# ConvFFN of a two-layer encoder trunk: the down product as seven block products in a phase of its own

## The reference, cut to what matters

```
def conv_ffn(h, w_up, conv_w, conv_b, w_down):
    u = h @ w_up                                  # (1024, 1024) @ (1024, 5632)
    u = causal depthwise conv of width 3 over the tokens (u, conv_w) + conv_b
    gate, val = split(u, 2)                       # 2816 channels each
    return (silu(gate) * val) @ w_down            # (1024, 2816) @ (2816, 1024)
```

## Time and profile before

| | |
|---|---|
| median of three runs | 2635.62 us |
| span of the profiled execution, first to last instruction | 2631.1 us |
| PE busy | 2439.2 us, 93% of the span |
| DVE busy | 1926.0 us, 73% |
| POOL busy | 1462.1 us, 56% |
| ACT busy | 846.4 us, 32% |
| moved by the DMA queues | 191.97 MB, 73 GB/s |

### The profile page before, as it was taken

How to read it: one execution, slowest core, us unless ns; L and a number is a source line. 1 busy time by engine, 2 the same in 40 slices (tenths; PEclk the granted TensorE clock), 3 DMA queues, 4 the chain that set the end, 5 groups by cost and what they waited for, 6 DMA issues and landing times.

```text
span 2631.1 us, 31515 instructions
## 1 busy us (share of the span) xinstructions
PE 2439.2 (93%) x11916; PEld 1957.4 (74%) x11916; DVE 1926.0 (73%) x2195; ACT 846.4 (32%) x1439; POOL 1462.1 (56%) x1123
## 2 busy tenths in 40 slices
PE   7899999989999999996899999978989999999993
PEld 5688887777777777773677787757777777777772
DVE  3676673796888888789666777662796788888878
ACT  3344451451111111114346465652441111111112
POOL 2222114547888888884441323114546888888883
PEclk9999999999999999998999999978999999999997
...
GB/s 153 56 65 73 60 134 152 147 30 57 49 49 48 57 49 61 52 88 102 53 65 39 87 52 80 18 160 120 128 57 51 54 49 48 49 57 48 57 63 104
DMA packets 51236, 191.97 MB, mean 73 GB/s; under 512 B 5904, under 2 KB 6416, under 8 KB 47376
## 3 DMA queue, kind: packets, MB, share of 16 engines
...
## 4 chain that ended last, share of the span: by engine, by line
PE 73%; DVE 16%; ACT 4%; issue 3%; DMA 2%; SPq 1%; ACTq 0%; POOL 0%; POOLq 0%; DVEq 0%
PE ps L1208 9%; PE ps L1209 9%; PE ps L1210 9%; PE ps L1230 6%; PE ps L1231 6%; PE ps L1232 6%; PE ps L1039 3%; PE ps L1011 2%; PE ps L1013 2%; PE ps L1012 2%; PE ps L1076 2%; PE ps L1056 2%; PE ps L1131 1%; PE ps L996 1%; PE ps L1133 1%
## 5 line engine op out<-in xcount | busy, mean ns | idle before, releaser
L2079 DVE TENSOR_TENSOR a<-a,ps 128x1024 f32<-128x1024 f32 x336 | 409.4, 1220 | 196.7 <-PE ps L1232 188.5
L748 POOL CAST w_hi<-w_raw 128x1024 fp32r<-128x1024 f32 x78 | 84.9, 1088 | 801.8 <-PE ps L1013 274.8
L1230 PE MATMUL ps<-hid,ring 128*128 128x512 f32 x704 | 294.7, 419 | 30.0 <-DVE a L2079 16.7
L1575 ACT ACTIVATE cy<-cx,cv 128x1024 f32<-128x1024 f32 x76 | 94.8, 1247 | 675.4 <-DVE cx L2050 675.4
L830 POOL TENSOR_TENSOR ring<-w_raw,ring 128x512 fp32r<-128x512 f32 x206 | 298.6, 1449 | 16.5
L1231 PE MATMUL ps<-hid,ring 128*128 128x512 f32 x704 | 278.1, 395 | 0.0
L1232 PE MATMUL ps<-hid,ring 128*128 128x512 f32 x704 | 277.0, 393 | 0.0
L828 POOL CAST ring<-w_raw 128x512 fp32r<-128x512 f32 x206 | 167.9, 815 | 184.2 <-PE ps L1232 92.8
L1209 PE MATMUL ps<-h,ring 128*128 128x512 f32 x608 | 237.2, 390 | 0.0
L1208 PE MATMUL ps<-h,ring 128*128 128x512 f32 x608 | 237.1, 390 | 0.0
L1210 PE MATMUL ps<-h,ring 128*128 128x512 f32 x608 | 236.8, 389 | 0.0
...
## 6 DMA issues: line engine op xcount, KB each, us to landing
w_raw<-in_W SPq DMA_DIRECT2D x166, 512.0 KB, 3.2
raw_d<-in_W SPq DMA_DIRECT2D x44, 512.0 KB, 3.2
...
```

The source lines that it names most:

```text
L1230: pe.matmul(out, wh, xh, start=True, stop=False)
L2079: dve.tensor_tensor(a[:, f, :], a[:, f, :], src, ALU.add).then_inc(acc_done, 1)
```

## The change

The down product becomes seven block products too. Two hidden tiles (a pair, 11 of them) by two halves of the output tiles by two halves of the tokens form the 2x2 blocks. Since the sums of hidden blocks need whole pairs, the mixer now runs in two phases.

- Phase 1 is the up product alone: three plain tiles, then 19 tiles of seven products. Finished hidden tiles go to DRAM (`store_hid`). POOL still casts and subtracts every item. Beside that it forms, for each pair, the four sums of the down weights (`pair_sums`, eleven times, at the tiles in `SUMS_BESIDE`); SP loads the pair (`load_pair`) and stores the sums to DRAM (`store_sums`).
- Phase 2 has 77 steps (7 products x 11 pairs), each one weight item and 12 matmuls into four accumulating banks. SP brings back the hidden tiles into `home` (`load_first`, `load_rest`) and each step's raw weights (`take_raw`, six places). ACT makes the tops of weights (`top`) and of hidden blocks (`operand_top`), POOL only subtracts the weights, DVE subtracts the hidden blocks (`operand_rest`) and forms their sums in place (`operand_sum`). Sums in `a` are made once per product (`evict`) instead of once per hidden tile.
- In phase 1 the products use banks 4 to 7, and convolution, silu and value are kept in banks 0 to 3 of PSUM instead of `cy`. The hidden tile is no longer split there (no `hid_top`, `hid_tail`). The last plain tile does its second token half first.
- x is reloaded in two halves during phase 2, and the first two weight units of the next stage are loaded after the last step's item (before: after items of the last tile).

PE has 10,368 instructions instead of 10,632 in the program.

```diff
+    out += [("up", 2, c) for c in ("g1", "v1", "g0", "v0")]
+    out += [("up", n, c) for n in range(PLAIN, HT) for c in PRODUCTS]
+    return out + [("dn", i, p) for i in range(len(DPRODUCTS)) for p in range(HP)]
...
+    out = [(n, c) for n in range(PLAIN) for c in ("G1", "G2", "V1", "V2")]
+    out += [(n, WEIGHT_OF[c]) for n in range(PLAIN, HT) for c in PRODUCTS]
+    return out + [("D", s) for s in range(len(DPRODUCTS) * HP)]
...
+    return {4 + (p * 18) // HP: p for p in range(HP)}
...
-return bank((len(PRODUCTS) * (n - PLAIN) + PRODUCTS.index(name)) % 4)
+return bank(4 + (len(PRODUCTS) * (n - PLAIN) + PRODUCTS.index(name)) % 4)
...
+    def store_sums(p):
+        sp.wait_ge(pair_sum, 4 * (HP * layer + p) + 4)
+        for k, src in enumerate((half_of(d_sum, 0, 0), half_of(d_sum, 0, 1), half_of(d_raw, 0, 1),
+                                 half_of(d_raw, 1, 0))):
+            sp.dma_start(sum_dram[layer, p, k, :, :], src).then_inc(sum_out, 16)
...
+    def take_raw(j):
...
+        if j >= DRAW:
+            sp.wait_ge(item_ready, item_count(layer, "D", j - DRAW))
+        sp.dma_start(taken(j), src).then_inc(take_in[j % DRAW], 16)
...
+    for n in range(PLAIN, HT):
+        if n in SUMS_BESIDE and SUMS_BESIDE[n]:
+            load_pair(SUMS_BESIDE[n])
+        if n + 2 < HT:
+            sp.wait_ge(item_ready, item_count(layer, n, "V2"))
+            load_raw(n + 2, "V")
+        store_hid(n - 1)
+        if n + 2 < HT:
+            sp.wait_ge(item_ready, item_count(layer, n, "S4"))
+            load_raw(n + 2, "G")
+        if n in SUMS_BESIDE:
+            store_sums(SUMS_BESIDE[n])
+            sp.wait_ge(sum_out, 64 * (HP * layer + SUMS_BESIDE[n] + 1))
+    for j in range(2):
+        take_raw(j)
+    sp.wait_ge(item_ready, item_count(layer, HT - 1, "S4"))
+    for j in range(2, DRAW):
+        take_raw(j)
+    sp.wait_ge(up_done, up_count(layer, HT - 1, "P5"))
+    for p in range(3):
+        load_first(p)
+    load_first(3)
+    load_rest(0)
+    take_raw(6)
+    load_rest(1)
+    load_rest(2)
+    sp.wait_ge(up_done, up_count(layer, HT - 1, "P3"))
+    for p in range(4, 8):
+        load_first(p)
+    take_raw(7)
+    load_first(8)
+    load_first(9)
+    take_raw(8)
+    load_rest(3)
+    take_raw(9)
+    load_rest(4)
+    take_raw(10)
+    store_hid(HT - 1)
...
+        if j == 5 * HP + 8:
+            sp.wait_ge(op_lo, step_no(layer, 4, HP - 1))
+            load_x(0)
+    sp.wait_ge(op_lo, step_no(layer, 6, HP - 1))
+    load_x(1)
...
-    sp.wait_ge(item_ready, item_count(0, HT - 1, ("S4", "V2")[u]))
+    sp.wait_ge(item_ready, item_count(0, "D", len(DPRODUCTS) * HP - 1))
...
+    def rest(n, name):
+        hi, lo = item_parts(n, name)
+        src = taken(name) if n == "D" else raw_of(n, name)
+        if n == "D":
+            pool.wait_ge(later_hi, len(DPRODUCTS) * HP * layer + name + 1)
+        else:
+            if name[0] == "S":
+                pool.wait_ge(w_sum, 4 * ((HT - PLAIN) * layer + n - PLAIN)
+                             + {"S1": 1, "S3": 2, "S2": 3, "S4": 4}[name])
+            pool.wait_ge(up_done, up_count(layer, *FREE_AFTER[n, name][1:]))
+            pool.tensor_copy(hi, src).then_inc(item_hi, 1)
+            pool.wait_ge(item_hi, up_item_count(layer, n, name))
+        pool.tensor_tensor(lo, src, hi.bitcast(F32), ALU.subtract).then_inc(item_ready, 1)
...
+    def pair_sums(p):
...
+        if p:
+            pool.wait_ge(sum_out, 64 * (HP * layer + p))
+        pool.tensor_tensor(s1_, a21, a22, ALU.add).then_inc(pair_sum, 1)
+        pool.wait_ge(pair_sum, count + 1)
+        pool.tensor_tensor(s2_, s1_, a11, ALU.subtract).then_inc(pair_sum, 1)
+        pool.tensor_tensor(a21, a11, a21, ALU.subtract).then_inc(pair_sum, 1)
+        pool.wait_ge(pair_sum, count + 2)
+        pool.tensor_tensor(a12, a12, s2_, ALU.subtract).then_inc(pair_sum, 1)
...
+    for n in range(PLAIN, HT):
+        rest(n, "S3")
+        last_sum(n)
+        rest(n, "V2")
+        if n + 1 < HT:
+            sums(n + 1)
+        rest(n, "S4")
+        if n + 1 < HT:
+            rest(n + 1, "G1")
+            rest(n + 1, "S2")
+        if n in SUMS_BESIDE:
+            pair_sums(SUMS_BESIDE[n])
+        if n + 1 < HT:
+            rest(n + 1, "G2")
+            rest(n + 1, "S1")
+    for j in range(len(DPRODUCTS) * HP):
+        rest("D", j)
...
+    def down(i, p):
+        j = HP * i + p
+        at_ = ring[RING_SLOT["D", j]]
+        pe.wait_ge(item_ready, item_count(layer, "D", j))
+        pe.wait_ge(op_lo, step_no(layer, i, p))
+        if i == 1 and p == 0:
+            pe.wait_ge(hid_f, HT * (layer + 1))
+        xh, xl = operand_parts(i, p)
+        for f in ((1, 2, 3, 0) if j == 0 else range(4)):
+            if j == 0:
+                pe.wait_ge(c_sum, result_count(layer, HT - 1, "C21" if f else "C12"))
...
+            out = down_bank(i, f)
+            wh, wl = at_[:, 0, f * P:(f + 1) * P], at_[:, 0, HB + f * P:HB + (f + 1) * P]
+            pe.matmul(out, wh, xh, start=p == 0, stop=False)
             pe.matmul(out, wh, xl, start=False, stop=False)
+            last = pe.matmul(out, wl, xh, start=False, stop=p == HP - 1)
+            if p == HP - 1 and f < 3:
+                last.then_inc(dn_done, 1)
         last.then_inc(dn_done, 1)
...
+            act.wait_ge(c_sum, result_count(layer, n, "C21" if v else "C12"))
+            act.activation(bank(2 * v, 2), cx[:, 2 * (n % 2) + v, :], ACT.Identity, bias=bi, scale=w
+                           ).then_inc(tap2, 1)
...
+    def top(j):
+        act.wait_ge(take_in[j % DRAW], 16 * taken_count(layer, j))
+        sort, m_, what = FREE_AFTER["D", j]
+        if sort == "up":
+            act.wait_ge(up_done, up_count(layer, m_, what))
+        else:
+            act.wait_ge(dn_done, step_count(layer, m_, what))
+        act.activation(item_parts("D", j)[0], taken(j), ACT.Copy).then_inc(later_hi, 1)
+    def operand_top(j):
+        i, p = j // HP, j % HP
+        if j == 0:
+            act.wait_ge(up_done, up_count(layer, HT - 1, "P6"))
+        if j >= 4:
+            act.wait_ge(dn_done, step_count(layer, (j - 4) // HP, (j - 4) % HP))
+        if i == 0:
+            act.wait_ge(first_in[p % 4], 16 * pair_count(layer, p))
+        elif DPRODUCTS[i] in ("P6", "P4", "P5"):
+            act.wait_ge(op_sum, sum_count(layer, i, p))
+        act.activation(operand_parts(i, p)[0], operand(i, p), ACT.Copy).then_inc(op_hi, 1)
...
+    top(0)
+    top(1)
+    top(2)
+    operand_top(0)
+    top(3)
+    operand_top(1)
+    tap(HT - 1, 1)
+    top(4)
+    operand_top(2)
+    tap(HT - 1, 0)
+    operand_top(3)
+    steps = len(DPRODUCTS) * HP
+    for j in range(4, steps):
+        if j + 1 < steps:
+            top(j + 1)
+        operand_top(j)
+        if j == 5:
+            gate(HT - 1)
+            act.preload_act_table_set("natural_log_exp_and_others")
+        if j in (HP + 3, HP + 4):
+            first_copy(2 * (j - HP - 3))
+            first_copy(2 * (j - HP - 3) + 1)
...
+    def operand_sum(j):
+        i, p = j // HP, j % HP
...
+        if name == "P6":
+            dve.wait_ge(rest_in[p % 4], 32 * pair_count(layer, p))
+            dve.tensor_tensor(b12, b22, b12, ALU.subtract).then_inc(op_dif, 1)
+            dve.wait_ge(op_dif, HP * layer + p + 1)
+            dve.tensor_tensor(b11, b12, b11, ALU.add).then_inc(op_sum, 1)
+        elif name == "P4":
+            dve.tensor_tensor(b21, b21, b11, ALU.subtract).then_inc(op_sum, 1)
+        elif name == "P5":
+            dve.tensor_tensor(b11, b22, b11, ALU.subtract).then_inc(op_sum, 1)
+    def operand_rest(j):
+        i, p = j // HP, j % HP
+        hi, lo = operand_parts(i, p)
+        dve.wait_ge(op_hi, step_no(layer, i, p))
+        dve.tensor_tensor(lo, operand(i, p), hi.bitcast(F32), ALU.subtract).then_inc(op_lo, 1)
+    def evict(i, f):
+        c11, c12, c21, c22 = half_of(a, f, 0), half_of(a, f, 1), half_of(a, 4 + f, 0), half_of(a, 4 + f, 1)
+        src = down_bank(i, f)
+        dve.wait_ge(dn_done, step_count(layer, i, HP - 1, f))
+        if i == 1:
+            dve.wait_ge(acc_first, 4 * layer + f + 1)
+        for dst, base_ in {"P6": [(c12, c11)], "P7": [(c22, c12)], "P2": [(c11, c11)],
+                           "P4": [(c21, c22)], "P5": [(c22, c22), (c12, c12)],
+                           "P3": [(c12, c12)]}[DPRODUCTS[i]]:
...
+            dve.tensor_tensor(dst, base_, src, ALU.add).then_inc(acc_done, 1)
...
+        for name in ("C11", "W", "C22", "U3", "C21"):
             result(n, name)
-        result(n, "C21")
-        if n < HT - 1:
-            for f in range(KT):
-                add(n - 1, f)
+        if n == HT - 1:
+            operand_rest(0)
+            operand_rest(1)
...
+    for j in range(6, steps):
+        if j + 1 < steps:
+            operand_sum(j + 1)
+        operand_rest(j)
+        if j % HP == 2 and j // HP >= 2:
+            for f in range(4):
+                evict(j // HP - 1, f)
+        if j == 6 * HP + 3:
```

(56 more changed lines are left out.)

391 lines of the change are left out of this document (204 added, 187 removed).

## The result

The changed kernel takes 2640.98 us (median of 19 runs, 2633.47 to 2646.16), the kernel before 2635.77 beside it (19 runs): a ratio of 1.0017, 95% interval 1.0010 to 1.0024. I had forecast 2600. PE has 132 matmuls per layer less, and yet the kernel is 3 to 6 us slower. The page of the profile says that PE is less busy (2439.2 us before) and DVE, too (1926.0); the span is 2635.8 us against 2631.1.

The account below looks back on a forecast made before the run. POOL was to bound phase 1, PE phase 2. The first layer's scaling comes 18.7 us earlier; 2 x 18.7 - 1.5 = 35.9 us less gives a span of 2595, 2600 us by the runs, range 2575 to 2660.

Parts of the forecast that it names:

- Phase 1 goes to POOL: Phase 1: POOL needs 23.9 us per tile with a pair's sums, PE 19.05; about 42 us of waits per layer.
- Rivals 1 and 4: Phase 1: POOL keeps its present slower durations, about 2690 us (0.10); or POOL isn't the bound, 2516 us (0.05).
- 1 us more as DVE's rests of the token sums lie beside it: Head of phase 1: DVE's rests delay POOL's first items, up to V2 at 577.4, by only 1 us.
- Loads for POOL are asked for a tile earlier [...] I cost them at nothing: Phase 1: POOL's loads land in 3.2 us and were given no cost.
- The seam: Between phases 1 and 2: PE waits 7.3 us for the first hidden block, plus 1.6 us for a halved clock.
- Phase 2 "at nothing": Phase 2: 209.6 us of PE; P6's POOL and DVE exclusion and the loads cost nothing, range 0 to 20 us.
- Rival 2: Phase 2 is short of data: its first two products lose 8 to 20 us per layer, 2616 to 2640 us (0.15).
- Behind it: After the last matmul: about 6 us of sums and squares, then 3.6 us to the scaling, at 1202.3 against 1220.96.
- I count each term twice: Both layers: the second has the same program, so the first layer's gain of 18.7 us was doubled.
- Rival 3: Phase 1: PE's waits halve its clock, 35 us per layer, up to 2670 us if uncovered (0.08).

Follow-up runs that it names:

- e2: Changed kernel with POOL's 44 sums of pairs per layer left out and raw halves stored instead (another down product): 2539.8 us, ratio to before 0.9633.
- e3: Changed kernel with ACT making the casts of up weights from the fifth item of tile 3 on, POOL only subtracting: 2533.08 us, ratio to before 0.9597.
- e1: Changed kernel with tile 4's raw weights loaded earlier, once the rests of T1 and T3 are made: 2639.31 us, ratio to before 1.0012.
- e4: Changed kernel with the first four hidden blocks loaded ahead of the four raw items waiting for the last up item: 2634.40 us, ratio to before 0.9992.
- e5: Changed kernel with the squares at the mixer's end kept in PSUM instead of SBUF: 2637.68 us, ratio to before 0.9997.
- e8: Changed kernel with ACT asking for the 6 MB reload two steps later in the second attention stage: 2632.67 us, ratio to before 0.9985.

## Why the prediction was wrong

The terms of the first layer, from the last plain matmul to the scaling:

| term | forecast, us | measured | short by |
|---|---|---|---|
| to POOL's first sum of tile 4 | 8.0 | 15.7 | 7.7 |
| from there to the last up item | 395.7 | 397.1 | 1.4 |
| to the first matmul of phase 2 | 8.9 | 9.1 | 0.2 |
| phase 2 | 209.6 | 212.9 | 3.3 |
| to the scaling | 9.7 | 13.6 | 3.9 |
| sum | 631.9 | 648.5 | 16.6 |

- **Phase 1 goes to POOL: right.** POOL's 127 items, 72 sums and 44 sums of pairs cost 397.1 us for 395.7, at the bare durations; e2 and e3, which took 46 and 50 us out of phase 1, show that the 42 us of waits were there. Rivals 1 and 4 fall with it.
- **The step that failed first: "1 us more as DVE's rests of the token sums lie beside it", and "Loads for POOL are asked for a tile earlier [...] I cost them at nothing".** POOL needed 10.2 us to the end of V2, 3.1 over its bare 7.0, where I had allowed 1; and the one load that isn't asked for earlier, tile 4's, made it wait 5.55 more: 7.7 of the 16.6. I had the price of the first in hand: in the earlier trace rows T1's four rests, just ahead of these twelve, take 5.09 us where four sums of two SBUF tiles take 2.49. The Trainium skill, page "SBUF — State Buffer", section "SBUF: two separate sides", whose rule of exclusion I used to call phase 1 free, holds for these rests as well, which have two SBUF inputs; the traces agree (T2's rests: 2.49 us with POOL idle in e3, 3.97 in the changed kernel, 6.79 in e1).
- **The seam: right by luck.** The first hidden block landed 7.6 us after the last up item instead of 5.7, so the wait was 9.1 instead of 7.3; the 1.6 us of half clock that I had added to it made up for that, and came in phase 2. "Nothing in the trace loads 256 KB" left stores of this size, at 2.0 us, unused.
- **Phase 2 "at nothing": 3.3 us.** About 1.7 are half clock at its start (the first step takes 4.41 us instead of 2.72), which I had put into the seam. Some 2 us are in P6, six of whose steps take 3.02 to 3.06 us, between the following starts, where I had worked out 3.1 and then trusted the operand places to cover it. DVE has no gap there, and its sums and rests take 1.77 to 1.79 us beside POOL where 0.68 is the bare time:

```profile
1037.55 0.47 PE L1457 MATMUL ps<-b_op,ring 128*128 128x512 f32 x1 [0.18 <-DVE b_op L2352]
...
1040.57 0.47 PE L1457 MATMUL ps<-b_op,ring 128*128 128x512 f32 x1
```

```profile
1037.32 1.77 DVE L2339 TENSOR_TENSOR home<-home 128x512 f32<-128x512 f32 x1
...
1040.34 0.68 DVE L2339 TENSOR_TENSOR home<-home 128x512 f32<-128x512 f32 x1
...
1041.66 1.79 DVE L2352 TENSOR_TENSOR b_op<-home,b_op 128x512 fp32r<-128x512 f32 x1
```

- **Rival 2 falls:** the queue was full (363 GB/s from 990 to 1020), but PE had no wait for data beyond the seam. In e4, without the pause of the seam, late loads stood behind two waits, 1.1 us in all.
- **Behind it: 3.9 us.** "As before 3.6 us to the scaling" held, and the 6 us of sums took 10, as POOL works on the weights of the next stage beside them; I had taken 1.5 us back for that. e5 shows the cause. It was there before the change, too, and I took the bare price although the trace showed the other: two sums of squares beside the same work took 5.08 us.

```profile
1212.27 5.08 DVE L2136 TENSOR_TENSOR ss<-ss,sq 128x1024 f32<-128x1024 f32 x2
```

- **"I count each term twice":** the second layer of before ended 3.1 us quicker than the first (9.3 against 12.4), so there was less to gain. With its mixer's own 12.5 us this makes 15.6 of the 16.7 that are missing there; 1 us is left over.
- **Rival 3:** PE's granted clock in phase 1 was 0.96 to 0.97; in the first layer it fell to half (1.2 GHz) in eight stretches, against some 20 waits for POOL. It cost nothing beyond the head, as POOL worked without a gap and set the pace. The Trainium skill, "TensorE: Matmul & The Clock Gate", section "HAM oscillation — how this bites in real kernels", tells of waits that throttle the array in every round; the trace agrees that the clock falls among such waits, but not after each, and the 35 us that the prediction worked out by it were not lost. In e2 and e3 the clock is 1.00 from 620 to 920 us without a change to PE's work.
- **What no rival named:** 6 us in a stage whose code is the same. Most of it is the late swap (with e8's edit DVE's wait there fell from 5.77 to 1.53 us); the rest stays open. Two forecast mixers less 2 x 16.6, and 6 more: that is the way from -36 to about +3, where the ratio gives +2.6 to +6.3.

The forecast of two clear gains rested on a small difference, 18.7 of 722 us, between two large sums, and every term at an edge was counted at its cheapest.
